# Prompt attention with four units in flight and another order of its query tiles

## The chip, the core and the metric

The kernel runs on one core of a Trainium2 chip. The metric is the time of one execution on the device in microseconds; a comparison uses the median of several executions of each kernel. The core has TensorE (PE, with PEld for its weight loads), VectorE (DVE), ScalarE (ACT), GpSimd (POOL) and SyncE (SP), each with a queue that it works off in order; they wait for one another by semaphores that are written into the program.

## What is computed

One layer of a decoder for a prompt of 1024 tokens and a sample group of 8 x 4 tokens. Each layer has a recurrent half and an attention half with three branches. For the prompt, the attention half comes down to this (8 heads in 2 groups that share keys and values, 64 columns a head):

```python
o_c, imp = cmp_attend(q, ckv, pos)               # compressed: 16 blocks of 64 rows, softmax over blocks
o_s = sel_prompt(q_rot, pos, idx, valid, kvs)    # selected: at 16 of 16 blocks this is plain causal attention
o_w = window_prompt(q_rot, kvw)                  # window: the last 512 keys
attn = g[:, :, 0] * o_c + g[:, :, 1] * o_s + g[:, :, 2] * o_w
merged = concatenate([rmsnorm(o_r, gn_rnn), rmsnorm(attn, gn_attn)])
```

After it come the same for the sample group (with paged caches), the output projection and a gated feed-forward block, and a final product with the weights for all rows.

## The kernel before

The program runs in stages: loads and conditioning, projections and the recurrence, keys and values, prompt attention, sample attention, and a trunk with the output projection and the feed-forward block. The change lies in `prompt_attention` (line 1523), which the trace shows from about 437 to 711 us.

**Trips, tiles, units.** There are four trips, one for each pair of heads `i` and `i + 4` (`KA` is 4). A trip goes over 8 tiles of 128 queries; for each tile there are four units: branch 1 (causal, `br` 1) and branch 2 (window, `br` 2), each for two heads `h`. `order` (line 1540) lists the 128 units, 32 in a trip, with tiles 0 to 7 in ascending order. A unit of tile `t` covers `t + 1` key tiles in branch 1 and at most 5 in branch 2, so tiles 0 to 3 have units of 1 to 4 key tiles, and tiles 4 to 7 have units of 5 to 8 (branch 1) and of 5 (branch 2).

**One unit.** PE makes the scores (`qk`, lines 1731 to 1737: two products per half and the masks) into PSUM at `place[n]`. VectorE takes the negative row maximum (`top`, 1917). ScalarE makes the exponential into `probs[n % 3]` and its sum (`exp`, 1819). VectorE takes the reciprocal of the sum (`weigh`, 1936). GpSimd scales the row by it and by the gate (1682). PE transposes the key tiles into PSUM bank 4 (up to four, line 1746) and bank 5 (the rest, 1753). ScalarE copies bank 4 into `pT[n % 4]` (`copy`, 1829), VectorE copies bank 5 (1926). PE then makes the weighted sums for two units at once (`weighted`, 1764 and 1772), and ScalarE takes a finished tile out of bank 6 or 7 (`take`, 1837).

**Depth.** Scores lie in banks 0 to 3: `place` gives even units banks 0 and 1 and odd units banks 2 and 3, whatever their size. So the scores of unit n wait for the exponential of unit n - 2. There are three probability buffers. PE's step n is: scores of n, transposes of n - 3, and at odd n the weighted sums of units n - 5 and n - 4. ScalarE's step n is: copy of n - 3, exponential of n, and on some steps the work below. The transposes of a unit wait for the copy of the unit before (`copied0`), since bank 4 is there once.

**Work beside the units.** At fixed steps of each trip stand the compressed softmax of the next trip (PE scores at step 3 into bank 5, `compress_scores`; VectorE's shift at step 4; ScalarE's exponential at step 4, line 1842; VectorE's weighing at step 6, lines 1899 to 1903; PE transposes at step 9; VectorE's copy at step 10) and the preparation of queries in halves (`stage` on VectorE, lines 1875 and 1878, and `double` on ScalarE, 1808: the second half of this trip at step 3, the first half of the next at step 19). For trip one, the first compressed softmax, the split of the keys in two parts (line 625; the second part at step 1) and the copy `compress_copy(0)` (line 1910) come at the start. GpSimd adds squares of finished tiles (`square`, 1666 to 1669) in trips two and four, and PE sums them at the end (1799).

## Time and profile before

| | us |
|---|---|
| median of 3 runs | 1695.3 (1693.31 to 1696.21) |
| the profiled execution | 1691.85 |
| its span, first to last instruction | 1690.0 |
| prompt attention in it, first scores to last sum taken | 442.8 to 710.5 |

The profile is one execution. Its page gives the busy time of each engine and the costliest groups of instructions; queries of the trace give waits (who waited for whom, and how long in total), windows (busy time and granted clock by stretch) and timelines (single instructions, with the idle time before each and what ended it). A start in the timeline is a time in microseconds from the span's first instruction. L1731 is line 1731 of the kernel.

### The profile page before, as it was taken

How to read it: one execution, taken by the hardware profiler on the slowest of the kernel's cores; microseconds unless marked ns; L12 is line 12 of the kernel's file. 1: busy time of each engine (PE TensorE's matmuls, PEld its weight loads, DVE VectorE, ACT ScalarE, POOL GpSimd, SP SyncE). 2: the span in 40 equal slices, each digit the busy share in tenths (PEclk: the TensorE clock that was granted, in tenths of full speed). 3: DMA queues.
4: the chain of work that ended last, by engine and by line, in shares of the span. 5: the costliest groups of instructions: out<-in, count | busy, mean ns of one | idle time of the engine just before them, and what ended most of it. 6: DMA issues, size and time to landing. Idle time of an engine off the chain costs nothing.

```text
span 1690.0 us, 29646 instructions
## 1 busy us (share of the span) xinstructions
PE 1604.8 (95%) x11172; PEld 1480.8 (88%) x11172; DVE 885.8 (52%) x1471; ACT 769.2 (46%) x1227; POOL 455.4 (27%) x553
## 2 busy tenths in 40 slices
PE   6998999999799999898899999999999999999997
PEld 5687888887687888755899999999999999999997
DVE  3666576675656655456675444434454434444433
ACT  5455255434577677532444554323354422354321
POOL 4222000142354545510653040033050033000032
PEclk9999999999699999888999999999999999999999
DMA  9942555235310001165544545345545455446442
GB/s 338 321 162 54 167 174 147 59 91 142 133 51 1 1 2 58 39 253 199 158 125 129 145 132 142 111 139 150 148 124 157 117 144 157 131 126 173 120 134 90
DMA packets 303165, 221.49 MB, mean 131 GB/s; under 512 B 21189, under 2 KB 289525, under 8 KB 298902
## 3 DMA queue, kind: packets, MB, share of 16 engines
q1 hardware_dynamic: 295412, 179.30, 36.8%
q0 software_dynamic: 7104, 40.76, 6.5%
q8 instruction: 65, 1.06, 0.3%
q14 instruction: 38, 0.31, 0.1%
q10 hardware_dynamic: 546, 0.05, 0.0%
HBM read 212.53 MB, written 11.68 MB: 133 GB/s over the span
## 4 chain that ended last, share of the span: by engine, by line
PE 49%; DVE 1%; ACT 1%; issue 0%; DVEq 0%; ACTq 0%; PEldq 0%
PE banks L629 16%; PE banks L631 16%; PE banks L630 16%; DVE ff_lo L625 1%; ACT ff_hi L621 0%; DVE hT L2852 0%; PE banks L2589 0%; ACT ff_h_hi L621 0%; DVE streams L2913 0%; ACT L621 0%; PE banks L2671 0%; DVE spare_rows L625 0%; ACT merged_hi L621 0%; PE banks L2580 0%; PE banks L2576 0%
## 5 line engine op out<-in xcount | busy, mean ns | idle before, releaser
L625 DVE TENSOR_TENSOR ff_lo<-ff_raw,ff_hi 128x2048 fp32r<-128x2048 f32 (+1 forms) x126 | 265.0, 2103 | 203.0 <-ACT ff_hi L621 202.8
L630 PE MATMUL banks<-low_rows,ff_hi 128*128 128x352 f32 x1120 | 359.0, 321 | 0.0
L629 PE MATMUL banks<-ff_h_hi,ff_hi 128*128 128x352 f32 x1056 | 341.5, 323 | 1.2 <-DVE ff_lo L625 1.2
L631 PE MATMUL banks<-ff_h_hi,ff_lo 128*128 128x352 f32 x1056 | 338.7, 321 | 0.0
L621 ACT ACTIVATE ff_hi<-ff_raw 128x2048 fp32r<-128x2048 f32 (+1 forms) x126 | 215.2, 1708 | 226.4 <-PE banks L631 212.2
L630 PEld LDWEIGHTS banks<-low_rows,ff_hi 128*128 128x128 f32 x1120 | 210.5, 188 | 0.3
L629 PEld LDWEIGHTS banks<-ff_h_hi,ff_hi 128*128 128x128 f32 x1056 | 198.0, 188 | 2.2 <-issue 2.0
L631 PEld LDWEIGHTS banks<-ff_h_hi,ff_lo 128*128 128x128 f32 x1056 | 198.4, 188 | 0.0
L629 PE MATMUL banks<-hid_hi,ff_hi 128*128 128x352 f32 x528 | 171.2, 324 | 4.3 <-DVE hid_lo L625 4.1
L631 PE MATMUL banks<-hid_hi,ff_lo 128*128 128x352 f32 x528 | 169.8, 322 | 0.0
L630 PE MATMUL banks<-hid_lo,ff_hi 128*128 128x352 f32 x528 | 169.4, 321 | 0.0
L1917 DVE TENSOR_REDUCE neg_max<-banks 128x1 f32<-128x640 f32 (+7 forms) x128 | 90.3, 706 | 93.7 <-PE banks L1736 89.1
L621 ACT ACTIVATE hid_hi<-streams 128x352 f32 (+1 forms) x66 | 32.9, 498 | 233.6 <-DVE streams L2913 233.6
L2913 DVE TENSOR_TENSOR streams<-streams,banks 128x352 f32<-128x352 f32 x66 | 34.4, 521 | 138.7 <-PE banks L631 138.6
L629 PEld LDWEIGHTS banks<-hid_hi,ff_hi 128*128 128x128 f32 x528 | 99.0, 188 | 5.4 <-issue 3.8
L629 PE MATMUL banks<-h_hi,s_hi 128*128 128x352 f32 x288 | 102.0, 354 | 1.5 <-DVE h_lo L625 1.5
L630 PEld LDWEIGHTS banks<-hid_lo,ff_hi 128*128 128x128 f32 x528 | 99.4, 188 | 0.0
L631 PEld LDWEIGHTS banks<-hid_hi,ff_lo 128*128 128x128 f32 x528 | 99.3, 188 | 0.0
L631 PE MATMUL banks<-h_hi,s_lo 128*128 128x352 f32 x288 | 93.7, 325 | 0.0
L630 PE MATMUL banks<-h_lo,s_hi 128*128 128x352 f32 x288 | 93.1, 323 | 0.0
L1682 POOL TENSOR_SCALAR hT<-hT,coef,gate_pair 128x640 f32<-128x640 f32 (+7 forms) x86 | 69.7, 810 | 81.3 <-DVE coef L1936 79.0
L1731 PE MATMUL banks<-k_halves,q_doubled 128*128 128x320 f32 (+4 forms) x192 | 79.7, 416 | 3.8 <-POOL tail_r L1640 1.8
(476 smaller groups left out, 3256.1 us busy)
## 6 DMA issues: line engine op xcount, KB each, us to landing
ff_raw<-in_w_gate SPq DMA_DIRECT2D x66, 512.0 KB, 4.0
ff_raw<-in_w_up SPq DMA_DIRECT2D x66, 512.0 KB, 5.3
ff_raw<-in_w_down SPq DMA_DIRECT2D x48, 384.0 KB, 4.1
late_ada<-in_w_ada SPq DMA_DIRECT2D x16, 1024.0 KB, 5.6
ff_raw<-in_w_down SPq DMA_DIRECT2D x48, 320.0 KB, 3.4
ff_raw<-in_w_out SPq DMA_DIRECT2D x24, 512.0 KB, 5.1
early_ada<-in_w_ada SPq DMA_DIRECT2D x4, 2048.0 KB, 22.7
s_raw<-in_w_in SPq DMA_DIRECT2D x48, 128.0 KB, 2.6
```

What stands on the lines that cost most here:

```text
L621: return act.activation(hi, raw, ACT.Copy)
L625: return dve.tensor_tensor(lo, raw, hi.bitcast(F32), ALU.subtract)
L629: pe.matmul(out, lhsT=w_hi, rhs=x_hi, start=first, stop=False)
L630: pe.matmul(out, lhsT=w_hi, rhs=x_lo, start=False, stop=False)
L631: return pe.matmul(out, lhsT=w_lo, rhs=x_hi, start=False, stop=last)
L1682: pool.tensor_scalar(probs[n % 3][:, 0:w], probs[n % 3][:, 0:w], coef[:, j], gsel[i % 2][:, t, br, h:h + 1], ALU.mult, ALU.mult).then_inc( ...
L1731: pe.matmul(psum[:, at + a:at + b], lhsT=QD[h][:, tile], rhs=KS[h][:, br - 1, keys], start=True, stop=False, skip_group_check=True)
L1917: dve.tensor_reduce(nmax[:, n % 4:n % 4 + 1], psum[:, place[n]:place[n] + w], AX, ALU.max, negate=True).then_inc(max_ready, 1)
L2913: dve.tensor_tensor(silu[p], silu[p], ps[2 * (1 - p) + 1][:, 0:GR], ALU.mult).then_inc(mixed, 1)
```

## The change

- The tiles of trips two to four are taken in the order 0 3 2 1 4 7 6 5 (`turns`); trip one keeps 0 to 7.
- A unit of up to four key tiles gets one bank of four (`u % 4 * 512`); a larger one keeps two banks, centred as before. `before[n]` is the latest earlier unit that uses one of its banks, and the scores wait for that unit's exponential.
- There are four probability buffers; the fourth lies in columns of `kvn` that hold window keys already stored. The wait for that store (`kv_stored`) moves from copy 0 to exponential 3.
- Transposes and copies follow the scores by four steps (`LAG`), the weighted sums by seven (`SUM_LAG`), and `take` and `square` by two steps more than before. The scores of units 0 to 3 are issued ahead of the loop.
- `compress_copy(0)` on VectorE moves from behind the first row maximum to step 1, behind the first reciprocal and ahead of the second part of the key split.

The core of the diff (`square`, and the loops over `turns` at the end, follow the new order in the same way):

```diff
-    order = [(i, t, br, h) for i in range(KA) for t in range(TILES) for br in (1, 2) for h in range(N_KV)]
+    turns = [range(TILES)] + [(0, 3, 2, 1, 4, 7, 6, 5)] * (KA - 1)
+    order = [(i, t, br, h) for i in range(KA) for t in turns[i] for br in (1, 2) for h in range(N_KV)]
...
-    place = [u % 2 * 1024 + (0 if len(x) <= 4 else 512 - len(x) * P // 2) for u, x in enumerate(tiles_of)]
+    place = [u % 4 * 512 if len(x) <= 4 else u % 2 * 1024 + 512 - len(x) * P // 2 for u, x in enumerate(tiles_of)]
+    banks = [{u % 4} if len(x) <= 4 else {u % 2 * 2, u % 2 * 2 + 1} for u, x in enumerate(tiles_of)]
+
+    before = [max([m for m in range(u) if banks[m] & banks[u]], default=None) for u in range(N)]
...
-    DONE = N + 4
+    LAG, SUM_LAG = 4, 7
+    DONE = N + SUM_LAG - 1
...
-        probs = [take_space(SEQ), take_space(SEQ), flat_kT[:, 0:SEQ]]
+        probs = [take_space(SEQ).rearrange("p (j n) -> p j n", n=P), take_space(SEQ).rearrange("p (j n) -> p j n", n=P),
+                 flat_kT[:, 0:SEQ].rearrange("p (j n) -> p j n", n=P), kvn[:, 0:TILES, 4 * KV_WIDTH:4 * KV_WIDTH + P]]
...
-                if n >= 10 and n % 4 == 2 and (n - 10) // 4 // TILES in (1, KA - 1):
-                    square((n - 10) // 4)
+                if n >= 12 and n % 4 == 0 and (n - 12) // 4 // TILES in (1, KA - 1):
+                    square((n - 12) // 4)
...
-                if n >= 2:
-                    pe.wait_ge(probs_ready, n - 1)
+                if before[n] is not None:
+                    pe.wait_ge(probs_ready, before[n] + 1)
...
-            qk(0)
-            qk(1)
+            for n in range(LAG):
+                qk(n)
             compress_turn(0)
             pe.wait_ge(v_spread, 16 * 4 * N_KV)
             for n in range(2, DONE):
                 i, u = trip_of(n)
-                if n < N:
+                if LAG <= n < N:
                     qk(n)
-                if 0 <= n - 3 < N:
-                    turn(n - 3)
+                if 0 <= n - LAG < N:
+                    turn(n - LAG)
...
-                if n % 2 == 1 and n >= 5:
-                    weighted((n - 5) // 2)
+                if n % 2 == 1 and n >= SUM_LAG:
+                    weighted((n - SUM_LAG) // 2)
...
             def exp(n):
                 act.wait_ge(max_ready, n + 1)
-                if n >= 3:
-                    act.wait_ge(turned0, n - 2)
-                    if second[n - 3]:
-                        act.wait_ge(turned1, upto[n - 3])
+                if n == 3:
+                    act.wait_ge(kv_stored, 16 * (5 + DEC_BATCH))
                 if n >= 4:
+                    act.wait_ge(turned0, n - 3)
+                    if second[n - 4]:
+                        act.wait_ge(turned1, upto[n - 4])
                     wait_scaled(act, n - 4)
...
             top(0)
-            compress_copy(0)
             for n in range(1, DONE):
...
                 if n == REST_AT:
+                    compress_copy(0)
                     split_keys(1)
```

## Rows read from the trace of the kernel before

**Rows 1.** The page, first part: busy us, share of the span, instructions.
```profile
PE 1604.8 (95%) x11172; PEld 1480.8 (88%) x11172; DVE 885.8 (52%) x1471; ACT 769.2 (46%) x1227; POOL 455.4 (27%) x553
```
**Rows 2.** Waits, 440 to 711 us: waiter, whom for, us, times, longest.
```profile
DVE neg_max L1917 <- PE banks L1736: 89.1, 76, 2.3
...
PE banks L1746 <- ACT kvn L1829: 3.6, 9, 1.4
```
**Rows 3.** Windows of 5 us: busy us (instructions) by engine, granted clock, DMA.
```profile
460.00:465.00 5.00, 5.00 (x28) 4.27 (x29) 1.95 (x7) 3.27 (x11) 2.39 (x7) 0.61 0.56 237
...
520.00:525.00 5.00, 3.35 (x25) 2.46 (x26) 3.74 (x14) 3.16 (x12) 1.52 (x3) 1.00 0.00 0
525.00:530.00 5.00, 4.78 (x28) 3.91 (x29) 2.64 (x10) 3.28 (x11) 1.82 (x4) 0.66 0.00 0
...
650.00:655.00 5.00, 4.20 (x31) 3.01 (x31) 2.96 (x11) 4.41 (x17) 2.68 (x5) 1.00 0.88 333
```
**Rows 4.** Timeline of PE: start us, us, instruction; first scores of tiles 0, 1, 3, 4.
```profile
510.12 0.39 PE L1731 MATMUL banks<-k_halves,q_doubled 128*128 128x256 f32 x1
...
519.78 0.38 PE L1731 MATMUL banks<-k_halves,q_doubled 128*128 128x256 f32 x1
...
532.17 0.50 PE L1731 MATMUL banks<-k_halves,q_doubled 128*128 128x512 f32 x1
...
538.60 0.41 PE L1731 MATMUL banks<-k_halves,q_doubled 128*128 128x320 f32 x1
...
640.30 0.38 PE L1731 MATMUL banks<-k_halves,q_doubled 128*128 128x256 f32 x1
...
648.20 0.38 PE L1731 MATMUL banks<-k_halves,q_doubled 128*128 128x256 f32 x1
...
658.05 0.50 PE L1731 MATMUL banks<-k_halves,q_doubled 128*128 128x512 f32 x1
...
664.48 0.42 PE L1731 MATMUL banks<-k_halves,q_doubled 128*128 128x320 f32 x1
```
**Rows 5.** Timeline of trip one's start, in brackets the idle time before and its releaser.
```profile
448.25 3.68 DVE L625 TENSOR_TENSOR k_halves<-kT,k_halves 64x1536 fp32r<-64x1536 f32 x2
...
450.65 3.46 PE L1701 MATMUL banks<-ck_pair,streams 128*128 128x32 f32 x16
...
453.93 0.56 PE L1731 MATMUL banks<-k_halves,q_doubled 128*128 128x256 f32 x1
...
456.93 0.42 DVE L1894 TENSOR_TENSOR cmp_probs<-cmp_probs,cmp_stat 128x256 f32<-128x256 f32 x1
...
457.38 0.42 ACT L1842 ACTIVATE cmp_probs<-cmp_probs 128x256 f32<-128x256 f32 x1 [1.07 <-DVE cmp_probs L1894]
...
458.11 0.45 PE L1746 MATMUL banks<-ident_m,hT 128*128 128x128 f32 x1 [0.28 <-ACT kvn L1829]
...
460.55 0.69 PE L1731 MATMUL banks<-k_halves,q_doubled 128*128 128x384 f32 x1
```
**Rows 6.** Timeline of trip two: transposes that waited, and VectorE's weighing, first and last instruction.
```profile
523.80 0.30 PE L1746 MATMUL banks<-ident_m,kT 128*128 128x128 f32 x1 [1.43 <-ACT kvn L1829]
...
524.23 0.40 DVE L1899 TENSOR_REDUCE cmp_stat<-cmp_probs 128x16 f32<-128x256 f32 x1
...
525.60 0.42 DVE L1903 TENSOR_TENSOR cmp_probs<-cmp_probs,cmp_stat 128x256 f32<-128x256 f32 x1
...
550.29 0.33 PE L1753 MATMUL banks<-ident_m,kT 128*128 128x128 f32 x1 [0.90 <-DVE kT L1926]
```
**Rows 7.** Groups by form (busy us, mean ns | idle before); then four transposes in the timeline.
```profile
L1829 ACT ACTIVATE kvn<-banks 128x512 f32<-128x512 f32 x60 | 35.9, 598 | 22.7 <-PE banks L1746 21.3
...
L1917 DVE TENSOR_REDUCE neg_max<-banks 128x1 f32<-128x512 f32 x16 | 11.1, 692 | 11.6 <-PE banks L1736 7.6 <-ACT hT L1819 3.1
...
701.50 0.63 PE L1746 MATMUL banks<-ident_m,hT 128*128 128x128 f32 x4 [0.34 <-ACT kT L1829]
```
**Rows 8.** Timeline of trip four's end: the last weighted sums, five key tiles.
```profile
705.67 1.31 PE L1772 MATMUL banks<-kvn 128*64 128x128 f32 x20 [0.58 <-ACT kvn L1829]
```

More of the change, by code:

```diff
@@ L1571, in prompt_attention @@
         flat_kT = kT[:, :, :].rearrange("p a n -> p (a n)")
-        probs = [take_space(SEQ), take_space(SEQ), flat_kT[:, 0:SEQ]]
+        probs = [take_space(SEQ).rearrange("p (j n) -> p j n", n=P), take_space(SEQ).rearrange("p (j n) -> p j n", n=P),
+                 flat_kT[:, 0:SEQ].rearrange("p (j n) -> p j n", n=P), kvn[:, 0:TILES, 4 * KV_WIDTH:4 * KV_WIDTH + P]]
         acc = take_space(SEQ)
         sq = take_space(P)
-        diag, tail = probs[0][:, 0:P], probs[0][:, P:2 * P]
+        diag, tail = probs[0][:, 0, :], probs[0][:, 1, :]
         pT = [kvn[:, 0:TILES, 2 * KV_WIDTH:2 * KV_WIDTH + P], flat_kT[:, SEQ:2 * SEQ].rearrange("p (j n) -> p j n", j=TILES)] + [
@@ L1658, in square @@
             def square(tile):
-                i, t = tile // TILES, tile % TILES
+                i, t, _, _ = order[tile * 2 * N_KV]
                 pool.wait_ge(taken, (tile + 1) * N_KV)
@@ L1671, in square @@
                         r.then_inc(squared, 1)
-                        pool.wait_ge(squared, t + 1)
+                        pool.wait_ge(squared, tile % TILES + 1)
                     else:
@@ L1678, in _ @@
                 if n < N:
-                    w, j = len(tiles_of[n]) * P, slice(n % 4, n % 4 + 1)
+                    w, j = len(tiles_of[n]), slice(n % 4, n % 4 + 1)
                     i, t, br, h = order[n]
                     pool.wait_ge(coef_ready, n + 1)
-                    pool.tensor_scalar(probs[n % 3][:, 0:w], probs[n % 3][:, 0:w], coef[:, j],
+                    pool.tensor_scalar(probs[n % 4][:, 0:w, :], probs[n % 4][:, 0:w, :], coef[:, j],
                                        gsel[i % 2][:, t, br, h:h + 1], ALU.mult, ALU.mult).then_inc(scaled, 1)
                     pool.wait_ge(scaled, n + 1)
-                if n >= 10 and n % 4 == 2 and (n - 10) // 4 // TILES in (1, KA - 1):
-                    square((n - 10) // 4)
+                if n >= 12 and n % 4 == 0 and (n - 12) // 4 // TILES in (1, KA - 1):
+                    square((n - 12) // 4)
                 if n < PER:
@@ L1745, in turn @@
                 for j in range(min(w, 4)):
-                    m = pe.transpose(ps[4][:, j * P:(j + 1) * P], probs[n % 3][:, j * P:(j + 1) * P], ident[:, :])
+                    m = pe.transpose(ps[4][:, j * P:(j + 1) * P], probs[n % 4][:, j, :], ident[:, :])
                 m.then_inc(turned0, 1)
@@ L1752, in turn @@
                     for j in range(4, w):
-                        m = pe.transpose(ps[5][:, (j - 4) * P:(j - 3) * P], probs[n % 3][:, j * P:(j + 1) * P], ident[:, :])
+                        m = pe.transpose(ps[5][:, (j - 4) * P:(j - 3) * P], probs[n % 4][:, j, :], ident[:, :])
                     m.then_inc(turned1, 1)
@@ L1794, in _ @@
                         compress_turn(i + 1)
-                if n % 2 == 1 and n >= 5:
-                    weighted((n - 5) // 2)
-            for t in range(TILES):
-                pe.wait_ge(squared, t + 1)
+                if n % 2 == 1 and n >= SUM_LAG:
+                    weighted((n - SUM_LAG) // 2)
+            for n, t in enumerate(turns[KA - 1]):
+                pe.wait_ge(squared, n + 1)
                 m = pe.matmul(ps[4][:, 2 * t:2 * t + 2], lhsT=acc[:, t * P:(t + 1) * P], rhs=ones[:, 0:2], start=True, stop=True)
@@ L1811, in exp @@
                 act.wait_ge(max_ready, n + 1)
-                if n >= 3:
-                    act.wait_ge(turned0, n - 2)
-                    if second[n - 3]:
-                        act.wait_ge(turned1, upto[n - 3])
-                w = len(tiles_of[n]) * P
+                w = len(tiles_of[n])
+                if n == 3:
+                    act.wait_ge(kv_stored, 16 * (5 + DEC_BATCH))
                 if n >= 4:
+                    act.wait_ge(turned0, n - 3)
+                    if second[n - 4]:
+                        act.wait_ge(turned1, upto[n - 4])
                     wait_scaled(act, n - 4)
-                act.activation(probs[n % 3][:, 0:w], psum[:, place[n]:place[n] + w], ACT.Exp,
+                act.activation(probs[n % 4][:, 0:w, :], psum[:, place[n]:place[n] + w * P].rearrange("p (j n) -> p j n", n=P), ACT.Exp,
                                bias=nmax[:, n % 4:n % 4 + 1], accum_out=den[:, n % 4:n % 4 + 1]).then_inc(probs_ready, 1)
@@ L1823, in copy @@
                 act.wait_ge(turned0, n + 1)
-                if n == 0:
-                    act.wait_ge(kv_stored, 16 * (5 + DEC_BATCH))
                 if n >= 4:
@@ L1851, in _ @@
                 i, u = trip_of(n)
-                if 0 <= n - 3 < N:
-                    copy(n - 3)
+                if 0 <= n - LAG < N:
+                    copy(n - LAG)
                 if n < N:
@@ L1861, in _ @@
                     double(i, 1)
-                if n % 2 == 0 and n >= 6 and order[n - 6][2] == 2:
-                    take((n - 6) // 2)
+                if n % 2 == 0 and n >= SUM_LAG + 1 and order[n - SUM_LAG - 1][2] == 2:
+                    take((n - SUM_LAG - 1) // 2)
         @block.vector
@@ L1957, in _ @@
                     weigh(n - 1)
-                if 0 <= n - 3 < N:
-                    copy(n - 3)
+                if 0 <= n - LAG < N:
+                    copy(n - LAG)
                 if n == REST_AT:
+                    compress_copy(0)
                     split_keys(1)
```

## The prediction

> **What bounds the kernel now.** I read the page first, then the waits of one stretch, then its windows, then its timeline. The page says that TensorE (PE) is busy for 95% of the span [rows 1]. That is a mean; the change lies in prompt attention alone, 442.8 to 710.4 us, so only that stretch is asked.
>
> The waits of the stretch show who is late. VectorE's row maximum waits 89.1 us for PE, and PE's transposes wait 3.6 us for ScalarE's copies [rows 2]. Mostly the other engines wait for PE, so PE is near its own work; what PE loses sits in few places.
>
> The windows show these places. From 520 to 525 us PE is busy for 3.35 of 5.00 us, and in the next window its clock is granted at 0.66: about 3.4 us at the 1.2 GHz level. The same place in trip four, 650 to 655, keeps 1.00. Trip one runs at 1.2 GHz until about 463.9 (0.61 of 460 to 465) [rows 3].
>
> The starts of the units give each trip's cost. Trip two takes 28.48 us for its first 16 units (tiles 0 to 3, 510.12 to 538.60); trip four, which has no compressed scores to prepare for a next trip, takes 24.18 us (640.30 to 664.48). Within that, tiles 1 and 2 take 12.39 us in trip two (519.78 to 532.17) and 9.85 in trip four (648.20 to 658.05) [rows 4]. The difference of 2.5 us, again in trip three, is the price of the next trip's compressed softmax.
>
> **The change part by part.** Three things set a step: PE's order is scores of unit n, then transposes, then, every second step, the weighted sums; ScalarE's is copy, exponential, then at step 4 the exponential of the compressed scores; VectorE's is maximum, reciprocal, copy, then at steps 3 to 6 the doubled queries, the shift and the weighing. All are in order.
>
> *Banks.* A unit of up to four key tiles gets one of four banks, so its scores wait for the exponential of n-4, not n-2. A unit of five or more still takes two banks and waits for n-2. So the second 16 units of a trip, more than half its work, gain no depth. One fence of `ps[4]` stays for all: transposes of n wait for ScalarE's copy of n-1.
>
> *Lag.* Transposes come a step later, the weighted sums two. That moves work but neither adds nor removes any: at unit 16 of trips two to four the new order has issued 54 transposes instead of 47 and sums over 29 key tiles instead of 25. Transposes follow each other every 0.11 us (four take 0.63, the last ends 0.30 after it starts) and a key tile of the sums takes 0.22 (five in 1.31, the last one ending 0.27 after it starts) [rows 7, 8], so 7 x 0.11 + 4 x 0.22 = 1.65 us lie in the first half which used to lie in the second. I add it to the old first halves before comparing.
>
> *Trip one.* PE can issue the scores of units 2 and 3 early, but VectorE's copy of the compressed probabilities now stands behind the reciprocal of unit 0, and the key split behind it. The split starts at 448.25 and takes 3.68 us [rows 5]; a copy of 0.4 us ahead of it makes it 448.7 to 452.4. The compressed scores on PE, 450.65 for 3.46 us, then start at about 448.8, and unit 4's scores at 452.4 instead of 453.93: 1.5 us early [rows 5]. But the gain is not kept. The shift's last instruction, 456.93, comes 0.6 late, at about 457.55; the exponential behind it (0.42) ends at 458.4 instead of 457.80, and the copy which PE needs is queued behind that. In the old order PE's third transposes start at 458.11 there [rows 5], those of unit 3; in the new one it is unit 2's, at 458.85 (copy 0.3 and 0.1 to start). PE then still owes one transpose (0.2) and the sums of units 0 and 1 (1.1, at 1.2 GHz): 0.75 + 1.3 = 2.05 us behind. Less 0.3 of waits before 460.55 that the old order had and the new has not, and 0.55 because the owed work shifts to 2.4 GHz: **+1.2 us**. At unit 19 VectorE prepares the next trip's queries, and in tile 5 PE waits 0.90 for the copy behind that [rows 6]; one more step of lag leaves about 0.5: **-0.4**.
>
> *Trips two and three, first half (0 3 2 1).* I walked the 16 steps with the durations of rows 4 to 7. Waits of PE come out so: 0.3 at step 1 and 0.4 at step 3 (a copy of four tiles, 0.60 [rows 7], behind only 0.4 us of scores); 0.5 at step 3, which is new: the next compressed scores share bank 5 with the last five-tile unit of the trip before, whose transposes now come at step 3 itself, so PE waits for VectorE's copy of them; 0.6 each at steps 6 and 7, where copies queue behind the compressed exponential as in the row of 523.80, which waited 1.43 [rows 6]; 0.2 and 1.3 at steps 8 and 9, since VectorE's weighing (1.8: 524.23 to 526.02 [rows 6]) delays the maximum of unit 7 (512 columns, 0.69 [rows 7]); 0.4 each at steps 11, 13 and 15. That is 5.1 on top of 25.35 of work and issue: 30.45 us. The old one is 28.48 + 1.65 = 30.1. **+0.4** for each trip. Tile 3 brings PE more work to put under VectorE, but it brings VectorE and ScalarE longer maxima, exponentials and copies as well, at the moment when these are late.
>
> *Second half (4 7 6 5).* The doubled queries at unit 19 now meet tile 7. Its maximum, twice as wide as the 0.69 of 512 columns, comes after them, and both the one-tile copy and the scores of unit 22 wait: by the same walk about 1.3, where tile 5's wait cost 1.1 (0.90 and the 0.2 until the transposes before it have ended). **+0.2** each in trips two and three.
>
> *Trip four and the tail.* The same walk without compressed scores gives 25.85, against 24.18 + 1.65 = 25.83: 0. At the end the last unit has five tiles in both orders; the wait of 0.58 before the last sums [rows 8] goes, and one of 0.7 between two transposes comes, since no scores lie between them: 0.
>
> *GpSimd, SyncE, addresses.* The fourth probability buffer lies in `kvn` with a stride; copies into such tiles (0.598 for 512 columns [rows 7]) are ScalarE's ordinary ones, so I take 0 for the layout; the bounds are 0 and, if a sixth of a copy is lost for each of its 32 units and nothing hides it, 3 us. GpSimd's squares move two steps later, with slack. No DMA is added; the wait for the key and value stores moves from copy 0 to exponential 3, at about the same time.
>
> Sum: 1.2 - 0.4 + 2 x 0.4 + 2 x 0.2 + 0 = **+2.0 us**. The profiled execution took 1691.85 (span 1690.0), so about 1693.9 for that; the median of the runs is 3.4 us higher, and on it 1695.3 + 2.0 = **1697.3 us**.
>
> **Rivals.** *The clock, slower.* The walk assumes 2.4 GHz throughout trips two and three and a return at 463.9 in trip one. By my walk PE waits about 3 us more there in 454 to 459 than it did. If the higher level comes back two stretches of 3.4 us later, half of 6.8 us is lost: 3.4. If the level falls in trips two and three as it did before [rows 3], that costs 1.0 to 1.4 each, because the walk has taken that loss out. Together 2.0 + 3.4 + 2.4 = 7.8: 1703.1. It decides from the point where PE's short waits between 455 and 461, or at steps 6 to 9, bring the 0.50 level. For it: the fall of 525 to 530 follows waits of which the longest is 1.43 [rows 6]. Against: 650 to 655, with 0.80 idle, kept its clock [rows 3], and the new waits are spread.
> The Trainium skill (TensorE: Matmul & The Clock Gate, Why this matters for your kernels) ties the fall to one idle gap longer than any in this stretch. By it this rival would cost 0 in trips two and three, and trip two would not have fallen before either. The trace disagrees: it fell, and the measurement decides.
>
> *Buffers were the limit, faster.* If four units in flight cover the compressed softmax and the doubled queries entirely, trips two and three cost what trip four costs: 2 x 2.5 [rows 4] and 2 x 1.0 for the doubled queries [rows 6], and trip one keeps its 1.5 [rows 5]: 8.5 us, 1686.8. For it: tiles 1 and 2 in trip four show that PE can run so. Against: the queue in front of the late copy is in order on ScalarE, which a bank doesn't shorten.
> The Trainium skill (Perfetto Trace Analysis, Optimization Strategy) says that a gap which repeats on the engine that should be saturated can mean too few buffers. By it the gain would be this rival's; the row of 523.80 names another cause, a copy queued behind an exponential, so I give it a minority.
>
> *It does nothing.* Where the tiles are large the depth stays two, and in the small ones the copy decides: 1695.3, inside my forecast's band.
>
> **How the numbers follow.** 0.2% is 3.4 us, about what a measurement of this kernel tells from no change. The forecast with its own errors (each walk is good to about 1 us, four trips) and the idle case fall within that: 0.46. The clock rival and smaller sums of the same sign: 0.32 slower. The buffers rival and parts of it: 0.22 faster. The likeliest alone would be 1694 to 1700.5. The range for 8 in 10 reaches towards both rivals: 1687.5 to 1703.
>
> **What would show it.** In the new trace: unit 4's scores at about 452.4 and the second transposes after the exponential at about 458.9; in trips two and three PE idle before transposes with ScalarE's copy as releaser, and before the compressed scores with VectorE's copy; first halves of 30.4, 30.4 and 25.9 us; the level 1.00 in trips two and three. If the first halves are below 28 us, the queues were not the limit. If the clock at 525 to 530 or after 464 is below 1.00, the slower rival is at work.

## The result and the profile after

The changed kernel takes 1699.7 us (median of 8 runs, 1698.1 to 1706.7) against 1695.5 (8 runs) for the kernel before: ratio 1.0030, 95% interval 1.0017 to 1.0042, so 4.2 us or 0.25% slower. Run once more beside other kernels it took 1699.0 against 1695.0 (1.0028, 1.0017 to 1.0039). The profiled execution of the change took 1706.65 (span 1704.8), 7 us more than its own median; some 10 us of its distance to the execution profiled before lie ahead of and behind prompt attention, in work that the change doesn't touch. So only the stretch of prompt attention is compared: 442.84 to 709.97 before, 267.1 us, and 446.31 to 717.67 after, 271.4. The difference there is 4.2 us, as between the medians.

In the changed file the lines stand five or six lower: L1737 are the scores (L1731 before), L1752 the first four transposes, L1759 the fifth and later, L1707 the compressed scores, L1834 ScalarE's copy, L1931 VectorE's.

The page, first part (busy us, share of the span, instructions), answers to [rows 1]. The shares are the same within one per cent; the loss can't be seen here.

```profile
PE 1611.2 (95%) x11172; PEld 1487.8 (87%) x11172; DVE 886.5 (52%) x1471; ACT 768.2 (45%) x1227; POOL 453.7 (27%) x553
```

Waits of prompt attention, 444 to 719 us (waiter, whom for, us, times, longest), against [rows 2]:

```profile
DVE neg_max L1922 <- PE banks L1742: 88.6, 72, 4.5
...
PE banks L1752 <- ACT kvn L1834: 11.8, 24, 1.4
```

VectorE waits for PE as long as it did, though its longest wait is now 4.5 us instead of 2.3. PE's transposes wait for ScalarE's copies 24 times instead of 9, and 11.8 us instead of 3.6. (The line counts only copies into `kvn`, in both kernels.) So PE is further from its own work than before. Over the whole stretch, the kernel before first and the change second (us, busy us of each engine, mean granted clock, DMA), its length less PE's busy time is 16.6 and 22.5 us:

```profile
442.84:709.97 267.13, 250.52 (x2263) 216.38 (x2264) 155.25 (x398) 185.42 (x468) 137.45 (x218) 0.95 0.07 26
```
```profile
446.31:717.67 271.36, 248.88 (x2264) 215.55 (x2264) 155.68 (x398) 184.31 (x468) 134.68 (x218) 0.95 0.07 26
```

Whole trips, first scores to first scores: us, busy us of each engine (instructions), mean granted clock, DMA. First trips two to four of the kernel before, then of the change, then trips two and three of the change when it was profiled again.

```profile
510.12:575.36 65.24, 61.48 (x569) 53.24 (x567) 38.67 (x100) 46.13 (x117) 32.95 (x51) 0.97 0.01 2
575.36:640.30 64.94, 61.45 (x568) 53.11 (x566) 38.63 (x100) 45.60 (x117) 29.77 (x41) 0.97 0.01 1
640.30:709.97 69.67, 65.81 (x637) 56.82 (x636) 34.11 (x88) 47.54 (x123) 39.79 (x65) 1.00 0.09 36
```
```profile
511.33:579.64 68.31, 62.70 (x581) 54.29 (x579) 39.73 (x100) 45.85 (x117) 31.55 (x49) 0.98 0.01 1
579.64:646.63 66.99, 61.83 (x568) 53.28 (x566) 38.64 (x100) 45.29 (x118) 28.84 (x41) 0.97 0.01 1
646.63:717.67 71.04, 66.29 (x654) 57.63 (x652) 34.42 (x89) 47.85 (x122) 39.56 (x65) 1.00 0.10 35
```
```profile
508.51:575.25 66.74, 61.10 (x581) 52.72 (x579) 39.77 (x100) 45.86 (x117) 31.61 (x49) 1.00 0.01 1
575.25:642.21 66.96, 61.90 (x568) 53.38 (x567) 38.64 (x100) 45.30 (x118) 28.87 (x41) 0.97 0.01 1
```

Trip one went from 67.28 us to 65.02 (446.31 to 511.33), the others grew by 3.07, 2.05 and 1.37. Part of that is work handed over a trip's end. At unit 0 of trip two the change still owes 26 transposes and sums over 18 key tiles, where the kernel before owed 18 and 13; at 0.11 and 0.22 us each that is 1.98 us more. At the end of trips two and three, where tile 5 comes last, it is 22 and 16 against the same 18 and 13: 1.10 more. With that put back, the trips changed by -0.3, +2.2, +2.1 and +0.3. **All of the loss lies in trips two and three**, the only trips with the new order that also prepare the compressed softmax and the doubled queries of a next trip. PE stands idle for 5.6 and 5.2 us in them (length less busy time), against 3.8 and 3.5 before: 3.5 of the 4.2 us.

Windows of 5 us of the change, same columns, against [rows 3]:

```profile
460.00:465.00 5.00, 3.19 (x14) 2.58 (x15) 3.91 (x16) 2.74 (x11) 2.40 (x7) 0.50 0.49 210
465.00:470.00 5.00, 4.82 (x36) 3.84 (x35) 2.74 (x9) 3.72 (x13) 3.06 (x9) 0.91 0.49 210
...
515.00:520.00 5.00, 4.16 (x41) 3.66 (x37) 3.04 (x10) 3.45 (x10) 0.89 (x2) 1.00 0.01 2
520.00:525.00 5.00, 5.00 (x43) 4.56 (x43) 0.55 (x2) 0.12 (x1) 0.00 (x0) 0.66 0.02 3
525.00:530.00 5.00, 4.26 (x38) 3.08 (x37) 4.61 (x14) 3.42 (x12) 1.87 (x3) 1.00 0.00 0
585.00:590.00 5.00, 4.27 (x37) 3.97 (x39) 2.80 (x7) 3.21 (x10) 0.49 (x2) 0.87 0.00 0
590.00:595.00 5.00, 5.00 (x44) 3.99 (x41) 2.33 (x8) 1.15 (x4) 0.45 (x1) 0.79 0.00 0
```

The clock falls from 2.4 to 1.2 GHz again once in each of trips two and three, but earlier: it was down in 525 to 530 and is now down in 520 to 525, where PE is busy throughout. VectorE and ScalarE work 0.55 and 0.12 us in that window: they starve behind a slow PE. The kernel before has one fall in each of these trips too, so the falls by themselves are no difference between the kernels.

Timeline of trip two: PE with what it waited for, and one row of VectorE (start us, us, engine, line, instruction, in brackets the idle time before it and its releaser):

```profile
517.20 0.63 PE L1752 MATMUL banks<-ident_m,kvn 128*128 128x128 f32 x4 [0.37 <-ACT kvn L1834]
...
518.41 1.94 PE L1707 MATMUL banks<-ck_pair,streams 128*128 128x32 f32 x16 [0.48 <-DVE kvn L1931]
...
524.10 0.50 PE L1737 MATMUL banks<-k_halves,q_doubled 128*128 128x512 f32 x1
...
524.93 0.69 DVE L1922 TENSOR_REDUCE neg_max<-banks 128x1 f32<-128x512 f32 x1 [4.45 <-PE banks L1742]
...
533.14 0.63 PE L1752 MATMUL banks<-ident_m,hT 128*128 128x128 f32 x4 [1.38 <-ACT kvn L1834]
...
539.57 0.30 PE L1752 MATMUL banks<-ident_m,hT 128*128 128x128 f32 x1 [0.37 <-ACT kvn L1834]
...
554.95 0.33 PE L1759 MATMUL banks<-ident_m,hT 128*128 128x128 f32 x1 [0.85 <-DVE kvn L1931]
```

Three places stand out: step 3 (518.41 to 524.10: compressed scores and weighted sums, mostly at 1.2 GHz), the transposes of step 9 (1.38 us) and the fifth transpose beside tile 7's scores (0.85). The last two had forerunners of about the same size in the kernel before (1.43 and 0.90, [rows 6]). What is new is many short waits. In trips two and three together, the kernel before first and the change second, PE's transposes wait for ScalarE's copies into `kvn` (us, times, longest):

```profile
PE banks L1746 <- ACT kvn L1829: 2.5, 5, 1.4
```
```profile
PE banks L1752 <- ACT kvn L1834: 7.0, 13, 1.4
```

### The profile page after: what moved, and what is told of

It is laid out like the page before. It is cut to its first block, busy times and chain, and to the rows that moved or that the text cites. A ratio compares the mean times of both kernels' runs of the same rounds, so it can differ in the third digit from the quotient of the medians.

```text
span 1704.8 us, 29644 instructions
## 1 busy us (share of the span) xinstructions
PE 1611.2 (95%) x11172; PEld 1487.8 (87%) x11172; DVE 886.5 (52%) x1471; ACT 768.2 (45%) x1227; POOL 453.7 (27%) x553
## 3 DMA queue, kind: packets, MB, share of 16 engines
q1 hardware_dynamic: 295412, 179.30, 36.6%
## 4 chain that ended last, share of the span: by engine, by line
PE 49%; DVE 1%; ACT 1%; issue 0%; DVEq 0%; ACTq 0%; PEldq 0%
PE banks L629 16%; PE banks L631 16%; PE banks L630 16%; DVE ff_lo L625 1%; ACT ff_hi L621 0%; DVE hT L2857 0%; PE banks L2594 0%; ACT ff_h_hi L621 0%; DVE streams L2918 0%; ACT L621 0%; PE banks L2676 0%; DVE spare_rows L625 0%; ACT merged_hi L621 0%; PE banks L2585 0%; PE banks L2581 0%
## 5 line engine op out<-in xcount | busy, mean ns | idle before, releaser
L1737 PE MATMUL banks<-k_halves,q_doubled 128*128 128x320 f32 (+4 forms) x192 | 78.9, 411 | 1.8 <-POOL tail_r L1646 1.8
L439 PE MATMUL banks<-zt,w 128*128 128x256 f32 (+1 forms) x256 | 70.1, 398 | 7.9 <-DVE zt L492 4.3
```

The lines of the kernel that those rows point to most:

```text
L439: m = pe.matmul(ps[2 * g + c][:, 0:wide], lhsT=w1[n % 2][:, c, l, :], rhs=zt[s % 2][:, c, 0:wide], start=False, stop=False, skip_group_che ...
L1737: pe.matmul(psum[:, at + a:at + b], lhsT=QD[h][:, tile], rhs=KS[h][:, br - 1, keys], start=True, stop=False, skip_group_check=True)
```

## The experiments

The theory at the start (A): four units in flight are to blame, because the compressed scores of step 3 now stand behind the transposes of the last five-tile unit. Its rival (B): the order of the tiles is to blame. Times in the table are medians; the ratios are to the kernel before on the same chip, with a 95% interval; the last column is prompt attention in the one profiled execution, from the first scores to the last row sums (267.1 before, 271.4 for the change, 270.1 for the change profiled again).

| kernel | us | ratio | interval | prompt attention, us |
|---|---|---|---|---|
| four in flight, ascending tiles | 1694.5 | 0.9989 | 0.9975 to 1.0003 | 266.1 |
| new order, three in flight | 1699.0 | 1.0021 | 1.0007 to 1.0034 | 270.8 |
| change, compressed branch a step later | 1695.5 | 0.9998 | 0.9985 to 1.0011 | 264.0 |
| change, weighing spread | 1700.1 | 1.0024 | 1.0012 to 1.0037 | 270.7 |
| change, new order in second half only | 1696.1 | 1.0006 | 0.9995 to 1.0017 | 266.2 |
| change, new order in first half only | 1699.4 | 1.0030 | 1.0018 to 1.0042 | 272.5 |
| change, stage spread | 1696.3 | 1.0010 | 0.9998 to 1.0022 | 268.0 |
| change, unaltered, again | 1699.0 | 1.0028 | 1.0017 to 1.0039 | 270.1 |
| four in flight, ascending, branch later | 1688.3 | 0.9958 | 0.9943 to 0.9973 | 259.5 |
| the same, weighing and stage spread | 1688.1 | 0.9961 | 0.9946 to 0.9977 | 258.0 |
| change, branch later, both spread | 1689.5 | 0.9962 | 0.9948 to 0.9977 | 261.8 |
| before, both spread | 1690.2 | 0.9971 | 0.9958 to 0.9983 | 262.7 |

**1. Depth alone, and order alone.** Four units in flight with the tiles ascending in every trip:

```diff
-    turns = [range(TILES)] + [(0, 3, 2, 1, 4, 7, 6, 5)] * (KA - 1)
+    turns = [range(TILES)] * KA
```

> The changed kernel with the tiles ascending in every trip: four units in flight alone. Theory A (the lag is to blame: with four units in flight the compressed scores of step 3 stand behind the transposes of the last five-tile unit of the trip before, in either order): the clock falls inside or right behind step 3 in trips two and three as it did in the changed kernel (520.4 and 588.7 us there), and the time is 1698 to 1701 us, ratio to before 1.002 to 1.004. Theory B (the order is to blame: four-tile units right behind tile 0): no fall of the clock in step 3, time 1693 to 1696 us, ratio 0.999 to 1.000.

And the kernel before with the order alone (the squares and row sums follow it):

```diff
-    order = [(i, t, br, h) for i in range(KA) for t in range(TILES) for br in (1, 2) for h in range(N_KV)]
+    turns = [range(TILES)] + [(0, 3, 2, 1, 4, 7, 6, 5)] * (KA - 1)
+    order = [(i, t, br, h) for i in range(KA) for t in turns[i] for br in (1, 2) for h in range(N_KV)]
```

> The kernel before with the tiles of trips two to four in the order 0 3 2 1 4 7 6 5, three units in flight. Theory A (the lag is to blame): the compressed scores of step 3 stand behind the transposes of tile 0 as before, no new wait there; trips two and three take as long as before (65.2 and 64.9 us) or up to 1 us less, since the light tiles 0 to 2 no longer follow one another; 1693 to 1696 us, ratio 0.9985 to 1.0005. Theory B (the order is to blame): trips two and three take 67 to 68 us as in the changed kernel, 1698 to 1701 us.

Measured: 1694.5 and 1699.0 us. The depth alone costs nothing; the order alone costs 3.6 us (ratio 1.0021), most of the change's 4 to 5. Trips two and three by whole-trip windows (columns as above), depth alone and then order alone:

```profile
512.04:576.99 64.95, 61.73 (x568) 53.41 (x566) 38.22 (x100) 45.69 (x117) 31.50 (x49) 0.97 0.01 2
576.99:642.03 65.04, 61.82 (x569) 53.43 (x567) 38.29 (x100) 45.36 (x118) 28.83 (x41) 0.97 0.01 2
```
```profile
513.19:580.66 67.47, 62.27 (x579) 53.66 (x577) 39.33 (x100) 45.87 (x117) 32.66 (x50) 0.97 0.01 2
580.66:647.13 66.47, 61.46 (x569) 53.13 (x567) 39.15 (x100) 45.38 (x118) 29.71 (x42) 0.97 0.01 1
```

Theory A falls on the time, B holds. But B's reason falls too: with ascending tiles and four in flight step 3 is just as bad. Its compressed scores wait 0.47 us for VectorE's copy, as in the change, and the clock falls there (mean 0.97 in both trips). Step 3 is a price of the depth, which the depth pays back elsewhere; the order has a price of its own. In these two trips PE is idle for 3.2 and 3.2 us with the depth alone and for 5.2 and 5.0 with the order alone, against 3.8 and 3.5 in the kernel before: the order's price is waits.

**2. The compressed branch one step later.** All its parts move by one, so that its scores follow the one-tile unit of tile 0:

```diff
-    CMP_AT, SHIFT_AT, EXP_AT, PROBS_AT, TURN_AT, COPY_AT = 3, 4, 4, 6, 9, 10
+    CMP_AT, SHIFT_AT, EXP_AT, PROBS_AT, TURN_AT, COPY_AT = 4, 5, 5, 7, 10, 11
```

> The changed kernel with the compressed branch of the next trip one step later in all its parts (scores at step 4, shift and exponential at 5, weighing at 7, transposes at 10, copy at 11), so that its scores stand behind the one-tile unit of tile 0 and not behind the last five-tile unit. Theory A: the wait for VectorE's copy in front of the compressed scores (0.48 us) is gone, ScalarE's and VectorE's idle time of 4.9 and 4.5 us in step 3 falls below 3 us, the clock stays up in step 3; trips two and three are 1.5 to 2 us shorter each, 1695 to 1697 us. Rival C (the clock falls because the tiles at a trip's start are light, wherever the compressed scores stand): the fall comes within the next five steps at the same cost, 1699 to 1700 us.

Measured: 1695.5 us, 3.5 to 4.2 less than the change. Whole trips two and three, then PE at the new place:

```profile
510.99:575.64 64.65, 60.89 (x580) 52.77 (x578) 39.81 (x100) 46.03 (x117) 31.56 (x49) 1.00 0.01 2
575.64:639.30 63.66, 59.71 (x569) 51.84 (x567) 39.09 (x100) 45.45 (x118) 29.06 (x41) 1.00 0.01 2
```
```profile
520.28 0.28 PE L1752 MATMUL banks<-ident_m,hT 128*128 128x128 f32 x1
520.39 1.87 PE L1707 MATMUL banks<-ck_pair,streams 128*128 128x32 f32 x16
522.10 0.48 PE L1737 MATMUL banks<-k_halves,q_doubled 128*128 128x512 f32 x1
```

The compressed scores wait for nothing, and the level is 1.00 through both trips. Rival C would have had the fall within five steps; it didn't come. That part of theory A stands: the place of the compressed branch is worth 3.5 us or more, with the order as it is. It is the place of the whole branch, not of its scores alone: VectorE's weighing moved with them, and the wait of 1.38 us at step 9 is gone too (none of trip two's first half is over 0.4). The change was measured again on another chip than this kernel; by the ratios to the kernel before (0.9998 and 1.0028) the gain is 5 us. The traces have 7.4 us of prompt attention against the change's first profile and 6.1 against its second, within what the two intervals leave open.

**3. VectorE's weighing spread** over steps 6, 7 and 8 (sum; clamp, reciprocal and gate; product):

```diff
-                    if u == PROBS_AT:
-                        compress_weigh(i + 1)
+                    if PROBS_AT <= u < PROBS_AT + 3:
+                        compress_weigh(i + 1, u - PROBS_AT)
```

> The changed kernel with VectorE's weighing of the compressed branch (five instructions, 2.0 us, all in step 6) spread over steps 6, 7 and 8. Theory A (the 1.38 us that TensorE waits in front of the transposes of step 9 are VectorE's block: the maximum of unit 7 stands behind it, the exponential of unit 7 behind that, and ScalarE's copy of unit 4 behind the exponential): that wait falls below 0.5 us, trips two and three are about 1 us shorter each, 1697 to 1698.5 us. Rival D (the wait is the length of the chain maximum, exponential, scaling, transposes, copy, not the block): it stays above 1 us, or comes back within two steps, and the time is that of the changed kernel, 1699 to 1700 us.

The row that answers to 533.14 of the change:

```profile
532.08 0.63 PE L1752 MATMUL banks<-ident_m,hT 128*128 128x128 f32 x4 [0.37 <-ACT kvn L1834]
```

The wait falls from 1.38 to 0.37 us and doesn't come back within tile 2, which takes 6.8 us instead of 7.8. So the block of 2.0 us on VectorE was the cause of the wait, as theory A had it. The time is not theory A's but stays at 1700.1, where rival D had it. In the profiled execution the clock fell twice in trip two, which then took 68.60 us; the second fall stands beside tile 7, behind waits of 0.63 and 0.87 us that the unaltered kernel has there too without a fall. Whether that is what holds the median up in the other runs isn't shown.

**4. Half of the order at a time.** 0 1 2 3 4 7 6 5, then 0 3 2 1 4 5 6 7:

```diff
-    turns = [range(TILES)] + [(0, 3, 2, 1, 4, 7, 6, 5)] * (KA - 1)
+    turns = [range(TILES)] + [(0, 1, 2, 3, 4, 7, 6, 5)] * (KA - 1)
```

> The changed kernel with the tiles of trips two to four in the order 0 1 2 3 4 7 6 5: the new order in the second half of a trip alone. The kernel with four units in flight and ascending tiles stood at 1694.5 us; the changed kernel at 1699.7. Theory E (each half of the order costs something of its own; by the two traces the second half, tiles 5 to 7, is 1.9 us longer in trip two and 1.4 in trip three than with ascending tiles, and 0.2 shorter in trip four): 1697.0 to 1698.5 us, with the 8-tile unit next to VectorE's stage of step 19 and a wait there of over 0.8 us in front of the transposes of tile 4. Rival F (the whole price is that of the first half): 1694 to 1695.5 us.

```diff
-    turns = [range(TILES)] + [(0, 3, 2, 1, 4, 7, 6, 5)] * (KA - 1)
+    turns = [range(TILES)] + [(0, 3, 2, 1, 4, 5, 6, 7)] * (KA - 1)
```

> The changed kernel with the tiles of trips two to four in the order 0 3 2 1 4 5 6 7: the new order in the first half of a trip alone. Theory E (by the two traces tiles 0 to 4 are 1.4 us longer in trip two, 0.6 in trip three and 0.2 in trip four than with ascending tiles, because falling tiles put short scores beside long transposes whose copies out of the one bank then stand open): 1696 to 1697.5 us, with waits of 0.3 to 0.4 us for ScalarE's copy at every second unit of tiles 2 and 1. Rival F (the whole price is that of the first half): 1699 to 1700 us.

Measured: 1696.1 and 1699.4 us. Theory E (each half has its price) falls; rival F (all of it is the first half) holds within a microsecond. The medians leave some room: by the ratios to the kernel before, the second half alone costs 2.9 us more than the depth alone, which the two intervals just allow to be nothing. The traces show no such cost (266.2 us of prompt attention against 266.1). Trips two and three with the new first half alone:

```profile
511.30:580.32 69.02, 63.44 (x569) 54.80 (x567) 39.31 (x100) 45.69 (x117) 31.54 (x49) 0.95 0.01 1
580.32:647.12 66.80, 61.92 (x568) 53.45 (x566) 38.54 (x100) 45.32 (x118) 28.84 (x41) 0.97 0.01 1
```

E read the two traces tile by tile, and saw tiles 5 to 7 longer in the change. The length was there, the cause was not: with the first half falling, tile 5 in its old place is long too (11.6 us in trip two, of which about 1.5 is a second fall of the clock, and 9.5 in trip three, against 9.0 with ascending tiles), and with the second half falling alone tile 7 is not long for its size (9.2 us, against 10.4 in the change). Behind tile 1 the units of tile 4 have only two-tile transposes and sums beside them and pass in 5.8 us instead of 7.6, while VectorE's maxima of five tiles take 0.82 us as ever. So PE runs ahead there, VectorE has no time in hand, and its stage of the next trip's queries then keeps PE waiting. This is read from the traces; the next experiment tests its last part. The falling tiles have a small price without any block, too. The waits of trip four's first half, which has neither branch nor stage, of the change and of the kernel with depth alone:

```profile
PE banks L1752 <- ACT kvn L1834: 2.4, 7, 0.4
```
```profile
PE banks L1752 <- ACT kvn L1834: 1.0, 5, 0.4
```

Short scores (tiles 2 and 1) then stand beside the longer transposes of the tile before, and PE comes to the one bank of transposes while ScalarE still copies it out.

**5. That stage spread**: the two products in step 19, one low part in each of steps 20 and 21.

```diff
-                    if u == FIRST_HALF_AT:
-                        stage(i + 1, 0)
+                    if FIRST_HALF_AT <= u < FIRST_HALF_AT + 3:
+                        stage(i + 1, 0, u - FIRST_HALF_AT)
```

> The changed kernel with VectorE's stage of the next trip's first half (four instructions, 3.36 us in step 19 of trip two) spread: the two products in step 19, one low part each in steps 20 and 21. Theory G (the 0.85 us before the fifth transpose in step 21, and part of the 0.63 us before the first four, are VectorE's block of 3.36 us, with the maximum and the copy behind it): the time lost in the units of tile 7 falls from 2.05 and 1.65 us to about 1, and the time by 1 to 2 us, 1697.7 to 1698.7. Rival H (the maxima of eight tiles, 1.23 us each, take the room): no change, 1699 to 1700.5 us.

Measured: 1696.3 us, 2.7 less than the unaltered change on the same chip. PE beside tile 7:

```profile
549.05 0.63 PE L1752 MATMUL banks<-ident_m,hT 128*128 128x128 f32 x4 [0.64 <-ACT kvn L1834]
...
549.52 0.27 PE L1759 MATMUL banks<-ident_m,hT 128*128 128x128 f32 x1
```

The 0.85 us before the fifth transpose are gone, ScalarE's 0.64 before the first four has stayed, and tile 7 takes 9.5 and 9.0 us in trips two and three instead of 10.5 and 9.8 in the unaltered kernel. Theory G holds; the time fell by more than it asked for, and trip two of this execution had no fall of the clock (1.00, 65.82 us).

**6. The change again**, unaltered, beside the last three:

> The changed kernel once more, unaltered, beside the three others on one chip: 1699 to 1700.5 us, ratio 1.002 to 1.003; if it stands at 1696 or below, the differences between the kernels of this study are those of chips and not of kernels.

1699.0 us: the differences are those of the kernels. Its trace, shown above, has a fall of the clock in trip three but none in trip two (66.74 us instead of 68.31), so one fall costs about 1.6 us here, and the same program has it in one execution and not in another.

**7. What is left when the places are mended.** Four in flight, ascending, with the branch later; then the weighing and the stage spread as well; then all of that with the new order; last the kernel before with both spreads and nothing else. The edits are those above.

> Four units in flight, ascending tiles, and the compressed branch one step later. Theory J (what the later compressed branch gave in the new order, some 3.5 to 4 us, it gives in ascending order too, since in both it then stands behind the one-tile unit of tile 0): the clock stays up in step 3, trips two and three take 63 to 63.7 us, 1690.5 to 1692.5 us. Rival K (the gain belonged to the new order, whose four-tile units stood right behind tile 0): 1694 to 1695.5 us, as with four units in flight alone.

> As the kernel before this one, with VectorE's weighing (steps 7 to 9) and its stage of the next first half (steps 19 to 21) spread as well. Theory J: another 0.3 to 0.6 us from each of trips one to three for the wait of tile 5 (0.87 us lost with four units in flight and ascending tiles, 0.15 in the units of tile 6), and up to 0.5 for the wait of tile 2; 1688.5 to 1691.5 us, faster than the kernel before. Rival K: 1692 to 1694.5 us.

> The changed kernel, order and all, with the compressed branch one step later, the weighing spread (steps 7 to 9) and the stage spread (steps 19 to 21). Theory L (the new order costs through VectorE's blocks, which the light units 1 and the quick units of tile 4 don't cover; with the blocks spread it costs nothing but 0.5 us a trip for the copies): 1690 to 1693 us, within 2 us of the same kernel with ascending tiles. Rival M (the order costs by itself, wherever the blocks stand): 1694 to 1697 us, 3 us or more above the same with ascending tiles.

> The kernel before (three units in flight, ascending tiles, compressed branch at its old steps) with the weighing spread over steps 6 to 8 and the stage over steps 19 to 21. Theory N (the splits help whatever the depth; tile 5 lost 1.4 and 1.2 us in its second unit in trips two and three): 1692.5 to 1694 us. Rival O (with three units in flight the chain maximum, exponential, scaling, transposes is the wait, and the blocks only lie beside it): 1695 to 1696 us.

Measured: 1688.3, 1688.1, 1689.5 and 1690.2 us; all four beat both kernels, and the second has the shortest prompt attention, 258.0 us. Trips two and three of the first and of the third:

```profile
511.65:573.44 61.79, 59.76 (x569) 51.88 (x567) 38.42 (x100) 45.84 (x117) 31.49 (x49) 1.00 0.01 2
573.44:635.49 62.05, 59.93 (x569) 51.86 (x567) 38.65 (x100) 45.46 (x118) 28.88 (x41) 1.00 0.01 2
```
```profile
511.32:574.88 63.56, 60.47 (x581) 52.72 (x579) 39.76 (x100) 46.17 (x117) 32.36 (x49) 1.00 0.01 2
574.88:637.65 62.77, 59.41 (x568) 51.86 (x566) 39.02 (x100) 45.47 (x118) 30.09 (x41) 1.00 0.01 2
```

Theory J holds and was too modest: the later branch alone gives the ascending kernel 5 to 6 us. Of the two spreads on top of it the medians show nothing (1688.1 against 1688.3), though the trace is 1.5 us shorter. On the kernel before the spreads alone give 5 us, more than theory N asked for: N's direction holds, rival O falls. Its trace says which of the two spreads it was. The second halves of trips one to three (from tile 4 on) take 35.6 us each instead of 36.6 to 36.8, and no wait over 0.2 us is left in them: 3.0 us from the stage. The wait of 523.80 in [rows 6] (1.43) and its like in trip three (1.54) have stayed in spite of the spread weighing:

```profile
523.33 0.30 PE L1746 MATMUL banks<-ident_m,kT 128*128 128x128 f32 x1 [1.42 <-ACT kvn L1829]
...
586.22 0.30 PE L1746 MATMUL banks<-ident_m,hT 128*128 128x128 f32 x1 [1.55 <-POOL kT L1682]
```

The other 1.4 us by which prompt attention is shorter are a fall of the clock that stayed away in trip two (first half 27.11 us instead of 28.48); whether the spreads kept it away isn't shown. The kernel before with its branch one step later was not run, so how much of the 7 us of the first kernel needs the fourth unit in flight is open. On the order with everything mended, L and M can't be told apart: the time is just below L's range and the medians differ by 1.4 us, within L, while the traces differ by 3.8 in prompt attention (261.8 against 258.0), as M would have it; the intervals are 5 us wide.

## Why the prediction was right or wrong

**The forecast** was 2.0 us slower; 4.2 were measured, inside the range of 1687.5 to 1703 and just past the 0.2% that the forecast stayed within. Depth and order were priced in one walk, and the walk did not show that one of them is free and the other is not. Term by term, with the work handed over put back:

| term | forecast, us | measured, us |
|---|---|---|
| trip one | +0.8 | -0.3 |
| first halves of trips two and three | +0.4 each | +1.7 and +1.8 |
| second halves of trips two and three | +0.2 each | +0.5 and +0.2 |
| trip four and the tail | 0 | +0.3 |

That the sum is off by no more than 2.2 us is in part luck: trip one erred by 1.1 us the other way. The count of the work handed over was short as well. By the trace an old first half has 46 transposes, not 47, and trip two of the change has 58 and sums over 31 key tiles, because trip one ends with tile 7; so 2.6 us move into the first half of trip two and 1.8 into those of trips three and four, where the walk had 1.65.

**Trip one, +1.2 - 0.4: too high.** With the work handed over put back, the trip changed by -0.3, and by 0.0 in the second profile. Rows of the change that answer to [rows 5]:

```profile
452.04 3.59 DVE L625 TENSOR_TENSOR k_halves<-kT,k_halves 64x1536 fp32r<-64x1536 f32 x2
...
452.15 3.60 PE L1707 MATMUL banks<-ck_pair,streams 128*128 128x32 f32 x16 [1.60 <-DVE cmp_turned L1915]
...
455.56 0.56 PE L1737 MATMUL banks<-k_halves,q_doubled 128*128 128x256 f32 x1
...
461.81 0.45 PE L1752 MATMUL banks<-ident_m,kT 128*128 128x128 f32 x1 [2.29 <-ACT kT L1834]
```

The chip reached this stage 3.5 us later in this execution, so times are counted from the first scores (442.84 and 446.31). Unit 4's scores start at 9.25 instead of 11.09: 1.8 early, forecast 1.5. The transposes behind the compressed exponential start at 15.5 instead of 15.3, 0.2 late; forecast 0.75 and one transpose and two sums owed on top. The mechanism is the one described, a gain at the front that is lost behind the queue; its size was overrated, because the whole time owed was counted as loss.

**Trips two and three, first half, +0.4 each: wrong in size, and this is the step that failed.** It was to take 30.45 us; it took 32.77 and 31.95. PE's first scores of tiles 0 and 4 in the two trips:

```profile
511.33 0.38 PE L1737 MATMUL banks<-k_halves,q_doubled 128*128 128x256 f32 x1
...
544.10 0.41 PE L1737 MATMUL banks<-k_halves,q_doubled 128*128 128x320 f32 x1
...
579.64 0.39 PE L1737 MATMUL banks<-k_halves,q_doubled 128*128 128x256 f32 x1
...
611.59 0.41 PE L1737 MATMUL banks<-k_halves,q_doubled 128*128 128x320 f32 x1
```

Most waits were listed rightly: 0.4 and 0.5 at step 3 (measured 0.37 and 0.48 in trip two), 1.3 at step 9 (1.38), 0.4 at steps 11, 13 and 15 (0.36, 0.37, 0.38). Those of steps 6 and 7 were smaller (0.29 and 0.45 instead of 0.6 each), those of steps 1 and 8 didn't come, and PE's idle time is 4.1 us in all where the walk had 5.1. What the walk left out is the clock. It had counted the old loss as gone and put the fall's price into a rival, so that the forecast stood on 2.4 GHz throughout; the fall came back one place earlier, at about 1.6 us each time. With that taken off, trip two is 0.7 us over the walk, about the work of trip one that it had not counted (4 transposes and 2 key tiles, 0.9), and trip three is on it; and where the fall stayed away, in trip two of the second profile, the half took 31.18 us (508.51 to 539.69). The rival said that the clock would decide in trips two and three if the new waits brought it down; in part it was at work, though not through the waits it named, for the falls came at step 3. Its other half, a late return in trip one, did not happen: the window of 460 to 465 is still at 0.50, 465 to 470 is mostly up, 19.5 us into the stage as against 21.0 before (20.9 in the second profile).
The Trainium skill (TensorE: Matmul & The Clock Gate, Why this matters for your kernels) ties the fall to one long idle gap on PE. Here PE's idle gaps in the nine microseconds ahead of the fall of 520.5 are 0.37 and 0.48 us, and before the change the longest ahead of a fall was 1.54: no such gap stands there, so this rule doesn't account for these falls.

**Second half, +0.2 each: right in time, wrong in cause.** The halves take 35.5 and 35.0 us, 35.3 by the forecast (36.76 - 1.65 + 0.2). The wait beside tile 7 is there. But it was put down to tile 7's wide maximum. The halves of the order show that by the trace tile 7 in that place costs nothing unless tiles 3 2 1 stand ahead of it, and experiment 5 that the longer of its waits goes when VectorE's stage is spread, with the maximum as wide as before.

**Trip four and the tail, 0:** +0.3 measured; the first half 26.2 against 25.85. The layout's 0 holds: copies of 512 columns still take 0.60 us.

**Buffers as the limit** (the faster rival): the deeper queue alone gives 1.3 us at the medians, not to be told from none, and its promise of 8.5 was off as a reading of its cause. Yet its amount was there to be had: 7 us come when the branch of compressed scores moves by one step with the depth. The Trainium skill (Perfetto Trace Analysis, Optimization Strategy) says that a repeated gap can mean too few buffers; here the gap in tile 5 repeated in trips one to three of the kernel before (0.72, 0.90 and 0.72 us), and spreading VectorE's stage over three steps, without any buffer, took it away (experiment 7).

## What to carry to other kernels

More units in flight help only as far as every engine's own order lets them: look for the block of one engine's instructions (here VectorE's stage, 3.4 us) behind which the next unit's short instructions stand, and spread it over steps before adding a buffer. Not every block pays: spreading the weighing (2.0 us) took a wait of 1.38 us out of the changed kernel and left its median where it was, and in the kernel before it left the wait. After a change of lag, look up again what each hand-placed instruction now stands next to; here one set of constants raised by a step was worth 4 to 6 us, as much as the whole change cost. An order that lets work shrink from tile to tile puts short scores beside long transposes, and PE then waits for the copies; price depth and order by separate kernels.

## What the runs showed of the hardware

The length of PE's waits doesn't tell when TensorE's clock falls. In ten profiled executions with the compressed scores at step 3 (both kernels, the change again, and experiments 1, 3, 4, 5 and the last of 7), the mean granted clock of trips two and three was 0.98 or less in 17 of 20 trips; in the four with the branch one step later it was 1.00 in 8 of 8.

The falls in the first halves of these 17 trips are of two kinds. (Two more came in the second half of trip two, beside VectorE's stage, in experiment 3 and with the new first half alone in experiment 4.) With four units in flight the fall came in 12 of 14 trips, 1.5 to 2.9 us behind the start of the compressed scores, and in the nine microseconds ahead of it PE had waited no longer than 0.48 us at a time. With three in flight (the kernel before, the order alone, the kernel before with both spreads) it came in 5 of 6 trips, at units 6 to 8, 0.5 to 1.6 us behind a wait of 1.33 to 1.55 us.

But waits of that length were also passed without a fall: the 1.38 us at step 9 of the change, with the level at 1.00 for the next 55 us, and the 1.42 us in trip two of the kernel before with both spreads. And in trip two of the change profiled again the waits of step 3 (0.36 and 0.47) brought none. The 16 products of 32 columns that make up the compressed scores take as long at step 3 as at step 4 (1.94 and 1.87 us). What it is that brings the fall isn't shown.
